# Post-norms with three buffers for squares, and the sums of squares on GpSimd

## The reference

```python
def rmsnorm(x, g):
    return x * lax.rsqrt(jnp.mean(x * x, axis=-1, keepdims=True) + EPS) * g

f = swiglu(rmsnorm(h, ffn1_pre_g), ...)        # 528 columns
h = h + 0.5 * rmsnorm(f, ffn1_post_g)          # first post-norm, the mixer's projection follows
m = hybrid_mixer(rmsnorm(h, mix_pre_g), ...)
h = h + rmsnorm(m, mix_post_g)                 # second post-norm, the second FFN follows
f = swiglu(rmsnorm(h, ffn2_pre_g), ...)
h = h + 0.5 * rmsnorm(f, ffn2_post_g)          # third post-norm, the second block's first mixer follows
```

## Time and profile before

| | us |
|---|---|
| median of three runs | 2625.05 (2624.13 to 2629.8) |
| the profiled execution, its own time | 2624.12 |
| its span, first to last instruction | 2622.3 |
| TensorE busy | 2569.0 (98%) |
| VectorE busy | 1287.2 (49%) |
| GpSimd busy | 1007.5 (38%) |
| ScalarE busy | 936.4 (36%) |
| mean granted clock of TensorE | 0.998 of full speed |

### The profile page before, as it was taken

The page is one execution under the profiler, slowest core; times in us unless marked ns, Lnnn a source line. Parts: engine busy times, 40 slices in busy tenths (PEclk is TensorE's granted clock), DMA queues, the critical chain, the costliest instruction groups (busy, mean ns, idle before and its releaser), DMA issues.

```text
span 2622.3 us, 35089 instructions
## 1 busy us (share of the span) xinstructions
PE 2569.0 (98%) x13458; PEld 2126.9 (81%) x13458; DVE 1287.2 (49%) x1396; ACT 936.4 (36%) x1310; POOL 1007.5 (38%) x446
## 2 busy tenths in 40 slices
PE   9999999999999999999999999999999999999999
PEld 8999998956777778888777688888877678888887
DVE  4443104367446534420487866662175745666213
ACT  4222223186334342222465232222254643222223
POOL 4443443302223344444343444444443124444443
PEclk9999999999999999999999999999999999999999
DMA  4222232201112232223321232223222012222321
GB/s 173 88 88 79 83 99 85 81 11 57 56 55 75 73 104 96 94 78 95 97 80 57 72 102 98 97 96 105 96 81 89 25 46 98 97 96 96 104 97 64
DMA packets 66050, 220.57 MB, mean 84 GB/s; under 512 B 8289, under 2 KB 8545, under 8 KB 65826
## 3 DMA queue, kind: packets, MB, share of 16 engines
q1 hardware_dynamic: 63792, 216.99, 25.1%
q10 hardware_dynamic: 2162, 2.25, 0.3%
HBM read 216.58 MB, written 2.10 MB: 83 GB/s over the span
## 4 chain that ended last, share of the span: by engine, by line
PE 88%; DVE 7%; ACT 3%; issue 2%; DMA 0%; ACTq 0%; SPq 0%; DVEq 0%
PE PS L297 26%; PE PS L299 26%; PE PS L298 26%; DVE acc L511 1%; PE PS L2817 1%; ACT xh L485 1%; DVE h L582 1%; PE PS L1274 1%; PE PS L1629 1%; DVE xl L489 1%; PE PS L2798 0%; DVE sq L503 0%; PE PS L2836 0%; DVE mt L1818 0%; PE PS L1656 0%
## 5 line engine op out<-in xcount | busy, mean ns | idle before, releaser
L292 POOL TENSOR_TENSOR wlo<-wraw,whi 128x1024 fp32r<-128x1024 f32 (+2 forms) x425 | 1000.5, 2356 | 1552.6 <-ACT whi L285 1551.9
L297 PE MATMUL PS<-xh,whi 128*128 128x512 f32 (+2 forms) x2504 | 890.8, 356 | 20.7 <-DVE xl L489 13.1
L298 PE MATMUL PS<-xl,whi 128*128 128x512 f32 (+2 forms) x2504 | 879.5, 351 | 0.0
L299 PE MATMUL PS<-xh,wlo 128*128 128x512 f32 (+2 forms) x2504 | 879.4, 351 | 0.0
L285 ACT ACTIVATE whi<-wraw 128x1024 fp32r<-128x1024 f32 (+2 forms) x425 | 429.3, 1011 | 849.6 <-PE PS L299 837.9
L297 PEld LDWEIGHTS PS<-xh,whi 128*128 128x128 f32 (+1 forms) x2504 | 470.7, 188 | 95.0 <-DVE xl L489 19.3
L299 PEld LDWEIGHTS PS<-xh,wlo 128*128 128x128 f32 (+1 forms) x2504 | 471.2, 188 | 63.5 <-issue 0.2
L298 PEld LDWEIGHTS PS<-xl,whi 128*128 128x128 f32 (+1 forms) x2504 | 470.8, 188 | 59.8 <-issue 1.0
L297 PE MATMUL PS<-hid2h,whi 128*128 128x512 f32 x560 | 217.8, 389 | 0.0
L298 PE MATMUL PS<-hid2l,whi 128*128 128x512 f32 x560 | 217.8, 389 | 0.0
L299 PE MATMUL PS<-hid2h,wlo 128*128 128x512 f32 x560 | 217.8, 389 | 0.0
(11 more groups left out here) (420 smaller groups left out, 3288.0 us busy)
## 6 DMA issues: line engine op xcount, KB each, us to landing
wraw<-w_up_dram SPq DMA_DIRECT2D x96, 512.0 KB, 3.2
wraw<-w_dn_dram SPq DMA_DIRECT2D x48, 512.0 KB, 3.2
wraw<-w_f1gu_dram SPq DMA_DIRECT2D x44, 512.0 KB, 3.2
wraw<-w_f2gu_dram SPq DMA_DIRECT2D x44, 512.0 KB, 3.2
wraw<-w_hyin_dram SPq DMA_DIRECT2D x24, 512.0 KB, 3.2
wraw<-w_win_dram SPq DMA_DIRECT2D x18, 512.0 KB, 3.2
wraw<-w_gate_dram SPq DMA_DIRECT2D x16, 512.0 KB, 3.2
wraw<-w_pg_dram SPq DMA_DIRECT2D x16, 512.0 KB, 3.2
```

The source lines that it names most:

```text
L292: pool.tensor_tensor(wlo[:, s, 0:size], wraw[:, s, 0:size], whi[:, s, 0:size].bitcast(F32), ALU.subtract).then_inc(lo_done.s, 1)
L297: pe.matmul(out_, whi[:, s, a:b], xhi, start=start, stop=False, skip_group_check=True)
L298: pe.matmul(out_, whi[:, s, a:b], xlo, start=False, stop=False, skip_group_check=True)
L299: return pe.matmul(out_, wlo[:, s, a:b], xhi, start=False, stop=stop, skip_group_check=True)
```

## The change

In `s_post_raw` there are three buffers for squares instead of one, so that the square of tile t waits for the sum of tile t-3 and not t-1, and the eight `added` calls move from VectorE's function to a new function of GpSimd's. That function is appended to GpSimd's list when the post-norm's stage is, so between `pool_` of the down projection and `pool_` of the next projection. The eighth of the calls (t = 0) only counts the semaphore; seven add, on 528 columns once and on 512 columns twice. The other users of `raw_tile` keep one buffer and VectorE.

```diff
-        def raw_tile(tag, gain, dst, n=T, landed=False):
+        def raw_tile(tag, gain, dst, n=T, landed=False, squares=(sq,)):
...
             def squared(act, t):
-                if t:
-                    act.wait_ge(*summed(t))
+                if t and t + 1 > len(squares):
+                    act.wait_ge(*summed(t + 1 - len(squares)))
                 there(act, t)
-                act.activation((acc if t == 0 else sq)[:, 0:n], h[:, t, 0:n], ACT.Square).then_inc(sqd.s, 1)
+                act.activation((acc if t == 0 else squares[(t - 1) % len(squares)])[:, 0:n], h[:, t, 0:n],
+                               ACT.Square).then_inc(sqd.s, 1)
...
                     dve.wait_ge(*summed(t))
-                    dve.tensor_tensor(acc[:, 0:n], acc[:, 0:n], sq[:, 0:n], ALU.add).then_inc(summed.s, 1)
+                    dve.tensor_tensor(acc[:, 0:n], acc[:, 0:n], squares[(t - 1) % len(squares)][:, 0:n],
+                                      ALU.add).then_inc(summed.s, 1)
...
-            kept, summed, scaled_high, scaled_low, squared, squared_here, added = raw_tile(tag, next_gain, x_of(n), n)
+            squares = (sq, at(f"squareb{gain}", o_tmp + 4224, [P, TK]), at(f"squarec{gain}", o_tmp + 6336, [P, TK]))
+            kept, summed, scaled_high, scaled_low, squared, squared_here, added = raw_tile(tag, next_gain, x_of(n), n,
+                                                                                           squares=squares)
...
                     scaled_low(dve, t)
                     if t + 1 < DT:
                         add(t + 1)
-                    if t >= 1:
-                        added(dve, t - 1)
-                added(dve, DT - 1)
-            stage(pe, act, dve)
+
+            def pool(pool):
+                for t in range(DT):
+                    added(pool, t)
+            stage(pe, act, dve, pool)
             return summed
```

## The result

| | before | after |
|---|---|---|
| median of five runs, us | 2625.05 (2624.13 to 2629.8) | 2703.57 (2702.3 to 2706.26) |
| span of the profiled execution, us | 2622.3 | 2701.9 |
| TensorE busy, us | 2569.0 (98%) | 2582.1 (96%) |
| GpSimd busy, us | 1007.5 (38%) | 1034.9 (38%) |
| mean granted clock of TensorE | 0.998 | 0.980 |

The ratio of after to before is 1.0300 (95% interval 1.0286 to 1.0314). The change makes the kernel 78.5 us slower, where 2703.5 was forecast.

What follows compares the result with a forecast made beforehand. TensorE, 98% busy, was taken to bound the kernel, so late openings count: 26.7 + 26.6 + 25.2 = 78.5 us on 2624.1 gives 2702.6, median 2703.5 us, range 2682 to 2713.

Steps and rivals of the forecast that it cites:

- The queue: Each post-norm: the next stage's four splits stand behind GpSimd's adds; the second opening ends 26.6 us later.
- The place sums: The openings behind the three post-norms end 26.7, 26.6 and 25.2 us later, 78.5 us in all.
- the lower clock behind the last split: TensorE's opening after its idle time: 1.7 us added a place for the lower clock, bounds 0 and 3.4.
- The collision: In the post-norm, GpSimd's add delays VectorE's add, 1.13 us a turn, so a turn stays at 3.27 us.
- (a): GpSimd and VectorE do not collide in the post-norms: turns of 2.14 us, 20.3 us come off, 2683 us; chance 0.09.
- (b): The paced start leaves TensorE at 1.2 GHz through 29 tiles: another 18 us a place, 2757 us; chance 0.03.
- (c): Four splits done before the adds, adds do not collide, TensorE bound by its own 21.8 us: 2609 us; chance 0.02.
- (d): Splits in time but adds collide: last xl 1.1 us later a place, 2628 us, no measurable change; chance 0.03.
- The loads: SyncE's loads of the next four chunks move back 27 us and cost nothing, as their ScalarE copies come later.
- the later part: Behind the openings everything follows in the same order, with no slack that would give back any delay.

Runs made afterwards that it cites:

- the first experiment: The changed kernel, but GpSimd splits the next projection's four first chunks before it adds squares; measured 2627.71 us, ratio 1.0003 to the kernel before.
- the filled kernel: The changed kernel with 64 filler products instead of 10 ahead of the opening; measured 2704.18 us, ratio 1.0304 to the kernel before.

## Why the prediction was right

**The queue** was the forecast's large term: the splits of the next stage stand behind the adds and TensorE needs all four. Three runs bear it out from different sides: with the splits first 75.9 us come back, with a bare wait in the adds' place 76.8 us are lost without them (2688.11 against 2611.33), and with half of the splits ahead only the part comes back that half of the splits take.

**The place sums** were 26.7, 26.6 and 25.2 us, the trace has 26.75, 26.69 and 24.55. That they agree so closely is partly luck, as errors cancelled. At the second place: I took the first `xl` at its old distance, but with no split beside it VectorE's first scale is not held up, which gains 0.45 us (924.95 - 26.75 = 898.20 against 898.65). From there to GpSimd coming free are 23.2 us and not 23.75, as the turn is 3.21 us and not 3.27. The four splits take 9.29 us and not 9.44. Together that is 1.15 us too much. Against it, the lower clock behind the last split costs more than the 1.7 us I took over from the earlier trace rows: from the last split's first matmul to the marker are 27.96 us, of which 24 matmuls are 5.44 and 29 tiles at full speed 19.7, which leaves 2.8, or 1.1 too little in my sum. At the first and third places no chunk stands between, and 22.47 us (442.86 to 465.33) and 21.83 us (1355.05 to 1376.88) leave 2.8 and 2.1, so in the third the errors cancel less. The bound of 0 to 3.4 us held all three. The clock behind the last split of the second place, by stretch:

```profile
957.50:963.00 5.50, 5.49 (x13) 4.33 (x14) 0.00 (x0) 0.00 (x0) 0.00 (x0) 0.50 0.34 127
963.00:976.00 13.00, 13.00 (x59) 10.69 (x58) 0.00 (x0) 0.00 (x0) 0.00 (x0) 0.99 0.01 1
```

**The collision** was costed at 1.13 us a turn from a row of another stage, and measures 1.75 - 0.69 = 1.06. The adds take 1.31 us (512 columns) and 1.35 (528), where the line through two other sizes gave 1.27 and 1.31. The rule of the Trainium skill that I set beside it ("SBUF — State Buffer", on the shared port pair) agrees with the trace but for about 0.13 us: in the first experiment VectorE's add to `h` begins 0.11 us behind GpSimd's and ends 0.55 us behind it, where 0.68 would be left by the rule. My sum took the 0.55 us from the earlier trace rows and not the rule's whole instruction.

**The rivals.** (a), no collision, is excluded by the rows of 1.75 us. (b), the slow clock through all 29 tiles, did not come about: the clock is back at 0.99 from 963 on, 5.5 us behind the last split's first matmul. (c) and (d) needed the splits ahead of the adds. The first experiment builds just that, and then it is (d) that comes: priced at 2628, measured 2627.71, which the spread of the runs does not tell from no change. The gain of (c) is real (5.4, 5.4 and 5.1 us a place, where I had 5.6, 5.3 and 5.3) but needs the adds off GpSimd.

**The loads and the later part.** The loads that moved back cost nothing, as forecast: ScalarE's rows between the first and second places are 26.75 to 26.81 us later than before, and between the second and third 53.44. I expected no change behind the openings; the profiled execution shows 1.6 us of lower clock there. That the medians differ by the 78.5 us forecast, to the tenth, is therefore luck too: the three places account for 78.0 of it.

## What to carry to other kernels

An engine that is busy 38% of the time can have room in time but not in order: before work that waits is put on it, look up what stands behind it in its list and who is waiting for that. A wait alone held up the list here and cost 77 us. Then check whether the two engines can run beside each other at all on such operands. And where one buffer makes two engines take turns, try a second buffer alone before moving the work.

## What was not expected of the hardware

Filler matmuls ahead of the stall did not save the clock behind it once tiles trickled in. In the filled kernel TensorE was idle for 1.90 us behind the filler, ran its first tile at full speed, and was idle again for 1.29 us. From 950 on the granted clock was 0.50, and the other paced tiles of the second place ran at 1.2 GHz, one of some 1.2 us every 2.32 us, as they do in the changed kernel behind 25 us of idle time. At the third place the first two tiles still ran at full speed. The mean clock of the whole run (0.980 to 0.993) improved without any time being saved (2703.57 and 2704.18 us).
